# Up products of an MLP on values without 1/rms, and an attention stage with three banks for its projections

## The reference

```python
def rms_norm_2(x, g, eps=NORM_EPS):
    y = xf * lax.rsqrt(jnp.mean(xf * xf, axis=-1, keepdims=True) + eps)
    return y * g

# second_block, end of each layer l
    x = x + merged @ w_out[l]
    h2 = rms_norm_2(x, mlp_norm[l])
    x = x + jnp.square(jax.nn.relu(h2 @ w_up[l])) @ w_down[l]

# na_mixer, 16 heads of 64; the latents form a grid of 8 rows and 64 columns
    q_l, k_l, v_l = jnp.split(h_lat @ w_qkv, 3, axis=-1)
    q_c, k_c, v_c = jnp.split(h_ctx @ w_qkv, 3, axis=-1)
    # each query: a window of 8 x 16 keys with a bias, and all 256 context keys
    p = softmax([s_nb + bias, s_cx]);  o = p_nb @ v_win + p_cx @ v_c
```

## Time and profile before

| | |
|---|---|
| three timed runs | 4324.96 us median (4319.55 to 4326.48) |
| profiled execution | 4325.29 us, span 4323.5 us |
| mean granted PE clock | 0.935 |
| PE busy | 3888.6 us, 90% of the span |
| DVE busy | 1850.3 us, 43% |
| ACT busy | 1320.7 us, 31% |
| POOL busy | 432.1 us, 10% |
| DMA | 317 MB, 73 GB/s on the mean |
| chain that ended last | PE 74%, DVE 12%, ACT 6%, DMA 3%, POOL 2%, issue 2% |
| attention stage, 1348 to 1746 us | PE busy 342.1 of 398 us, clock 0.93 |
| entrance of the MLP, 2877 to 2903 us | PE busy 18.1 of 26 us, clock 0.74 |
| the same in layer 1, 3942 to 3968 us | PE busy 18.1 of 26 us, clock 0.74 |

### The profile page before, as it was taken

One profiled execution on the slowest core, in us unless ns is written; L12 is line 12 of the kernel. 1 busy time (PEld: TensorE's weight loads), 2 busy tenths in 40 slices (PEclk: granted clock), 3 DMA queues, 4 the chain that ended last, 5 costly groups with the idle time before them and its releaser, 6 DMA issues.

```text
span 4323.5 us, 52579 instructions
## 1 busy us (share of the span) xinstructions
PE 3888.6 (90%) x21392; PEld 3030.3 (70%) x21392; DVE 1850.3 (43%) x2826; ACT 1320.7 (31%) x1963; POOL 432.1 (10%) x277
## 2 busy tenths in 40 slices
PE   7788878999997899899978889899998888989999
PEld 3555546788886777688865667678886666767887
DVE  2543443533333334544444354543434435454433
ACT  3332322322223322333333331232232433123222
POOL 0211110000002110000021220000011122000000
PEclk9877878999998999899989999999999999999999
DMA  4112252121211222232211221123321121112332
GB/s 159 52 48 79 88 175 98 49 69 59 69 49 45 88 82 89 69 98 98 88 45 35 66 56 40 35 90 95 95 90 42 42 71 49 32 47 88 98 98 68
DMA packets 320320, 317.03 MB, mean 73 GB/s; under 512 B 8720, under 2 KB 286128, under 8 KB 319952
## 3 DMA queue, kind: packets, MB, share of 16 engines
q1 hardware_dynamic: 320080, 313.67, 23.0%
HBM read 311.55 MB, written 2.10 MB: 73 GB/s over the span
## 4 chain that ended last, share of the span: by engine, by line
PE 74%; DVE 12%; ACT 6%; DMA 3%; POOL 2%; issue 2%; SPq 0%; DVEq 0%; ACTq 0%; POOLq 0%
PE PS L132 74%; DVE scr L146 5%; ACT scr L142 4%; DMA ring<-in_ada_w 1%; DVE PS L160 1%; DMA scr<-in_na_bias 1%; DVE scr L156 1%; DVE NBt L156 1%; PE PS L135 1%; POOL na_w L146 1%; ACT L142 1%; DVE scr L164 1%; DVE scr L168 1%; DVE NBt L146 0%; POOL NBt L146 0%
## 5 line engine op out<-in xcount | busy, mean ns | idle before, releaser
L132 PE MATMUL PS<-scr 128*32 128x32 f32 (+7 forms) x6692 | 659.9, 284 | 131.0 <-DVE scr L146 72.8
L132 PEld LDWEIGHTS PS<-scr 128*128 128x128 f32 (+4 forms) x6692 | 538.7, 170 | 276.6 <-issue 122.5
L132 PE MATMUL PS<-ffn_h,ffn_w 128*128 128x512 f32 (+1 forms) x3168 | 616.2, 357 | 7.8 <-DVE ffn_h L156 5.7
L132 PEld LDWEIGHTS PS<-ffn_h,ffn_w 128*128 128x128 f32 x3168 | 524.8, 190 | 100.3 <-issue 9.1
L142 ACT ACTIVATE scr<-PS 128x256 f32<-128x256 f32 (+4 forms) x489 | 231.5, 473 | 1001.5 <-PE PS L132 920.6
L146 DVE TENSOR_TENSOR scr<-scr 128x512 f32<-128x512 f32 (+3 forms) x419 | 289.0, 690 | 257.9 <-ACT scr L142 221.8
L132 PE MATMUL PS<-h_h,ring_r 128*128 128x512 f32 (+1 forms) x976 | 356.1, 427 | 36.1 <-POOL ring_r L146 22.0
L132 PE MATMUL PS<-mlp_h,mlp_w 128*128 128x512 f32 x1536 | 364.3, 399 | 5.5 <-DVE mlp_h L146 5.0
L132 PE MATMUL PS<-mlp_g,mlp_w 128*128 128x512 f32 x1536 | 359.7, 396 | 0.0
L132 PEld LDWEIGHTS PS<-mlp_h,mlp_w 128*128 128x128 f32 x1536 | 291.2, 190 | 80.0 <-issue 9.5
L132 PEld LDWEIGHTS PS<-mlp_g,mlp_w 128*128 128x128 f32 x1536 | 288.5, 188 | 69.9
(11 more groups left out here) (150 smaller groups left out, 4709.6 us busy)
## 6 DMA issues: line engine op xcount, KB each, us to landing
ring<-in_ada_w SPq DMA_DIRECT2D x48, 1024.0 KB, 7.0
ring<-in_ffn_w_in SPq DMA_DIRECT2D x44, 1024.0 KB, 5.1
ring<-in_w_up SPq DMA_DIRECT2D x32, 1024.0 KB, 5.5
ring<-in_w_down SPq DMA_DIRECT2D x32, 1024.0 KB, 5.0
ring<-in_w_in SPq DMA_DIRECT2D x60, 512.0 KB, 3.9
ring<-in_ffn_w_out SPq DMA_DIRECT2D x16, 1024.0 KB, 5.1
scr<-in_na_bias SPq DMA_DIRECT2D x32, 512.0 KB, 5.5
ring<-in_na_w_qkv SPq DMA_DIRECT2D x24, 512.0 KB, 4.0
```

The costliest lines, as they stand in the source:

```text
L132: return self.eng.matmul(o, lhsT=l, rhs=r, start=start, stop=stop) if self.eng else Nothing()
```

## The change

In the MLP, `tail_act` writes `ms_at(k)[0]`, the high half of x times gain, right after each residual addition of the merge, and `tail_dve` the low half behind both additions of a group. `norm_dve` and `norm_act` are gone there. `products` gets an argument `half`, called ahead of its fifth chunk; for the first up group it is `rstd_pe`, and `rows_pe` comes behind that group. DVE copies the row into SBUF (`row`). An up tile leaves PSUM by one DVE operation, max with 0 and times row; ACT squares it and writes the high half; DVE writes the low halves after both tiles. The weight split of the second up group now stands ahead of the root and of the reciprocal.

In the attention, `flip(it)` writes into the two banks that held the scores of `it`, whose release is now the copy of the flipped probabilities; projections rotate through banks 4, 5 and 7. The order of the pieces is q, k latents, v latents, v context, k context, then the transposes of v. The split of the next q/k weights moves behind the context k on ACT and POOL, and SP makes three weight loads ahead and issues two at each `project`.

```diff
+    def products(pe, ring_, split, j, nk, segs, src, ready, full, freed, half=None):
...
         for k in range(nk):
+            if half and 2 * k == nk:
+                half()
             for t in range(nt):
...
-        for _ in range(4):
+        for _ in range(3):
             fetch()
 
         def project(tl):
             fetch()
             for _ in range(6):
-            if tl < 7:
-                fetch()
+            fetch()
...
-        s_ring, t_ring, o_ring = banks([0, 2], 2), banks([4, 5]), banks([6])
+        s_ring, o_ring = banks([0, 2], 2), banks([6])
...
-        def project(tl):
-            pe.wait_ge(*at("na_lo", "qk", tl))
-            for what, j, (t0, tn) in NQK:
+        def qk(tl, parts):
+            for what, j, (t0, tn) in parts:
...
+        def project(tl):
+            pe.wait_ge(*at("na_lo", "qk", tl))
+            yield from qk(tl, NQK[:2])
             wh, wl = w8(4096, 1024), w8(5120, 1024)
             pe.wait_ge(*at("na_lo", "v", tl))
             for s, (t0, tn) in enumerate(LC):
                 o, before = cur["rg"].take("na_made", "n_vt", tl, s)
                 emptied(pe, before)
                 for k in range(8):
...
+            yield from qk(tl, NQK[2:])
             for g in range(3):
...
-                cur["rg"] = banks([7])
-            o, before = s_ring.take("n_ex", it)
+                cur["rg"] = banks([4, 5, 7])
+            o, before = s_ring.take("n_pt", it, 1)
...
         def flip(it):
             z = it % 2
+            pe.wait_ge(*at("n_dg", it))
             for hf in range(2):
-                o, before = t_ring.take("n_pt", it, hf)
-                emptied(pe, before)
-                pe.wait_ge(*at("n_dg", it))
+                o = psum("n_pt", it, 1)[:, 512 * hf:512 * hf + 512]
                 for c in range(4):
                     t = pe.mm(o[:, c * 128:c * 128 + 128], Pm[z][:, hf, c * 128:c * 128 + 128], dg[z][:, hf, :], True, True)
                 t.then_inc(*pe.up("nt_full", it, hf))
...
-            for what, j, (t0, tn) in NQK:
-                yield
...
-            if tl < 7:
-                split_act("qk", tl + 1)
+            for what, j, (t0, tn) in NQK[:2]:
+                yield from qk(tl, what, j, t0, tn)
             for s, (t0, tn) in enumerate(LC):
...
+            what, j, (t0, tn) = NQK[2]
+            yield from qk(tl, what, j, t0, tn)
+            if tl < 7:
+                split_act("qk", tl + 1)
             for g in range(3):
...
-            o = psum("n_ex", it)
+            o = psum("n_pt", it, 1)
...
         def project(tl):
             split_pool("v", tl)
-            for _ in range(6):
+            for _ in range(10):
                 yield
             if tl < 7:
                 split_pool("qk", tl + 1)
-            for _ in range(10):
+            for _ in range(6):
...
+    row = acc[:, 0:TL]
...
-            if what == "up" and q == 0 and n == 0:
-                rstd_pe(pe, rg, f"p{l}", (LAT,), ("ss_p",))
-                rows_pe(pe, rg, f"p{l}", (LAT,))
+            first = what == "up" and q == 0 and n == 0
...
-            products(pe, rg, split, j, 8, (LOW,), src, ready, lambda t, s: (f"q{l}", j, t, s), q_freed(l, what, q, n))
+            products(pe, rg, split, j, 8, (LOW,), src, ready, lambda t, s: (f"q{l}", j, t, s), q_freed(l, what, q, n),
+                     (lambda: rstd_pe(pe, rg, f"p{l}", (LAT,), ("ss_p",))) if first else None)
+            if first:
+                rows_pe(pe, rg, f"p{l}", (LAT,))
...
         for j, (what, q, n) in enumerate(q_groups()):
             if what == "up" and q == 0 and n == 0:
+                split.act(act, j + 2)
                 rstd_act(act, f"p{l}", (LAT,))
-                norm_act(act, f"p{l}", (LAT,), None, ms_at)
             split.act(act, j + 2)
...
                 elif what == "merge" or what == "down" and q == 3 and l == 0:
                     st2 = f"p{l}" if what == "merge" else "a1"
                     act.wait_ge(*at("q_x", l, what, q, k))
+                    if what == "merge":
+                        act.f(ms_at(k, 0, TL)[0], XL[:, k, :], ACT.Identity, scale=V(f"mlp_norm{l}", k)).then_inc(*act.up("nh", st2, k, 0))
                     if k >= 3:
                         act.wait_ge(*at("ss_p", st2, k - 2, 0))
                     square_act(act, st2, k, 0, LAT, (k - 1) % 2)
                 elif what == "up":
-                    if n or q:
-                        act.wait_ge(*at("mlp_low", "q_lo", l, q if n else q - 1, (k - 2) % 8))
-                    act.f(upt[t], o, ACT.Relu).then_inc(*act.up("mlp_made", "q_up", l, what, q, k))
-                    act.wait_ge(*at("mlp_low", "q_c2", l, q, k))
+                    act.wait_ge(*at("mlp_low", "q_up", l, what, q, k))
+                    act.f(upt[t], upt[t], ACT.Square).then_inc(*act.up("mlp_made", "q_sq"))
                     if q:
                         act.wait_ge(*at(*last_down(l, q)))
                     act.f(mg_at(k, 0, TL)[0], upt[t], ACT.Copy).then_inc(*act.up("mlp_made", "q_hi", l, q, k))
...
             if what == "up" and q == 0 and n == 0:
+                split.dve(dve, j + 2)
                 rstd_dve(dve, f"p{l}", (LAT,))
-                norm_dve(dve, f"p{l}", (LAT,), lambda k, s: V(f"mlp_norm{l}", k), None, ms_at)
+                dve.wait_ge(*at("rs_full", f"p{l}", 0, "row"))
+                dve.cp(row, rstd_of(f"p{l}", 0, TL)).then_inc(*dve.up("nx", f"p{l}", 7, 0))
             split.dve(dve, j + 2)
...
                 elif what == "up":
-                    hi, lo = mg_at(k, 0, TL)
-                    dve.wait_ge(*at("mlp_made", "q_up", l, what, q, k))
-                    dve.tt(upt[t], upt[t], upt[t], ALU.mult).then_inc(*dve.up("mlp_low", "q_c2", l, q, k))
-                    dve.wait_ge(*at("mlp_made", "q_hi", l, q, k))
-                    dve.tt(lo, upt[t], hi.bitcast(F32), ALU.subtract).then_inc(*dve.up("mlp_low", "q_lo", l, q, k))
+                    dve.wait_ge(*at("pr_full", f"q{l}", j, t, 0))
+                    dve.stt(upt[t], psum(*q_freed(l, what, q, n)(t, 0)), 0.0, row, ALU.max, ALU.mult).then_inc(*dve.up("mlp_low", "q_up", l, what, q, k))
                 else:
...
+            for k in (2 * n, 2 * n + 1):
+                if what == "merge":
+                    hi, lo = ms_at(k, 0, TL)
+                    dve.wait_ge(*at("nh", f"p{l}", k, 0))
+                    dve.stt(lo, XL[:, k, :], V(f"mlp_norm{l}", k), hi.bitcast(F32), ALU.mult, ALU.subtract).then_inc(*dve.up("nl", f"p{l}", k, 0))
+                elif what == "up":
+                    hi, lo = mg_at(k, 0, TL)
+                    dve.wait_ge(*at("mlp_made", "q_hi", l, q, k))
+                    dve.tt(lo, upt[k % 2], hi.bitcast(F32), ALU.subtract).then_inc(*dve.up("mlp_low", "q_lo", l, q, k))
```

More of the change, by code:

```diff
@@ L370, in dve @@
                 self.made["dve"] = j + 1
-    def products(pe, ring_, split, j, nk, segs, src, ready, full, freed):
+    def products(pe, ring_, split, j, nk, segs, src, ready, full, freed, half=None):
         wh, wl = split.tiles(j)
@@ L1716, in na_act, with qk @@
         norm_act(act, "na", LC, ada_gain(1, 0, f_col)[1], na_parts)
+        def qk(tl, what, j, t0, tn):
+            yield
+            act.wait_ge(*at("na_in_full", "n_full", tl, j))
+            if tl >= 2:
+                act.wait_ge(*at("ns_full", 4 * (tl - 2) + 3))
+            act.f(QT[tl % 2] if what == "q" else KTt[tl % 2][:, t0:t0 + tn], psum("na_made", "n_in", tl, j)[:, 0:tn], ACT.Copy,
+                  scale=64 ** -0.5 if what == "q" else 1.0).then_inc(*act.up("na_made", "n_in", tl, j))
+            yield
         def project(tl):
```

17 lines of the change are left out of this document (6 added, 11 removed).

## The result

| | before | changed |
|---|---|---|
| median of the runs | 4323.39 us (4319.55 to 4326.48, 4 runs) | 4293.7 us (4290.82 to 4301.3, 4 runs) |
| ratio | | 0.9935, 95% interval 0.9921 to 0.9949 |
| profiled execution | 4325.29 us, span 4323.5 | 4293.35 us, span 4291.6 |
| mean granted clock | 0.935 | 0.939 |

The change makes the kernel 29.7 us faster. The forecast was 48.4 us faster, 4277 us, with a range of 4269 to 4289: the sign is right, the gain is 19 us too small (the time 17 us too long; the median of before came out 2 us lower than the forecast had it), and the time lies outside the range. The sign of being wrong that the forecast had named, a distance above 42 us in the attention, has come.

The account below looks back on a forecast made before the run. TensorE, busy 90% of the span, was taken to bound the kernel, so only its waits and half-clock stretches could pay: 4325.3 - 24.4 (MLP entrances) - 24.0 (attention) = 4276.9, said as 4277 us, range 4269 to 4289.

Parts of the forecast that it names:

- a distance above 42 us in the attention: Attention: the forecast is wrong if the distance between last value products of neighbouring head pairs stays above 42 us.
- The MLP's entrance: Both layers, PE free to second up group: 25.4 us falls to 13.2; gain 24.4 us for two (20.8 to 24.8).
- Rival B: MLP entrance: the wait returns inside the first group, half the gain is lost, 4289 us; chance 0.05.
- Steady up groups: nothing: MLP's later up groups: moving relu to DVE and the square to ACT costs nothing; 3 us if cover were gone.
- The loads: Attention: weight loads issued earlier no longer hold up bias loads, so every pair should look like the undisturbed one.
- the six distances: Attention, last value products of pairs one to seven: 264.67 us falls to 246.0, gain 18.7; lower bound 252.4, gain 12.3.
- The third bank: Attention, quarter four: v transposes need not wait for ACT's eviction; gains 1.07 us a pair of the 1.92 wait.
- the undisturbed pair: Attention: a head pair with no weight load left to issue, 42.07 us before, 41.0 forecast after the change.
- the place of POOL's split: Attention: q/k split one quarter later; POOL ends at 1675.1, PE wants it at 1677.8, margin 2.7 us, no cost.
- rival C: Attention: the q/k split moved one quarter later makes PE wait for POOL once per pair; slower, 4334 us; chance 0.03.
- new pair: 42.07 - 1.07 = 41.0: Attention: time per head pair after the change, the undisturbed pair less the third bank's gain; six make 246.0 us.
- the first pair: Attention's first head pair: last value products at 1449.1 against 1454.37, gain 5.3 us; 3.8 with half clock.

Follow-up runs that it names:

- the old order: Changed kernel with projections again q, both k, then v, and the q/k weight split back in the second quarter; 4266.44 us, ratio 0.9872.
- POOL in halves: Changed kernel with POOL's subtraction for the q/k low half cut into two instructions of half the columns; 4282.01 us, ratio 0.9914.
- the one-tensor diagonal: Changed kernel with the diagonal made by two products of the identity with a scalar per row, not one two-tensor product; 4295.86 us, ratio 0.9941.

## Why the prediction was right and wrong

**The MLP's entrance: right.** 12.55 us against 13.2. The sums took from 2873.68 to 2874.49, 0.81 (forecast 1.2), the row product 0.45 on PE's path (0.87). The gain is 25.7 against 24.4, above the upper end of 24.8 that the bounds gave. Rival B did not come: no idle row ahead of the sums. The margin for it was smaller than forecast: POOL's sum ended at 2872.84, 0.84 us ahead of PE's sums, not 1.3. "Steady up groups: nothing" holds to 0.7 us for both layers together, and the operation that takes the relu out of PSUM on DVE took 1.49 us for two (from 2882.04 on), the 0.748 of the earlier trace rows each. What the sum lacked is the 2.4 us in the unchanged code between the two MLPs.

**The loads: right in the mechanism.** SP's new order removes every wait of DVE for the bias, and the kernel with this alone shows it by itself: 16.5 us in the stage. In size it is right only together with the banks: alone it brought 6.0 of the 12.3 us that the forecast gave the six distances, because the wait for ACT that it leaves is followed by slow value products in four of six pairs.

**The third bank: right in size, with the cover named.** "The third is not worth its 1.92 us", 1.07 of it; the undisturbed pair came out at 40.94 to 40.97 against 41.0 and the remaining wait at 0.97 against 0.9, once the fault below is out of the way. What the forecast did not see is that a gone wait also takes away the half clock that sometimes followed it.

**The step that failed: the place of POOL's split, under rival C.** The forecast asked one question of the move by a quarter, whether POOL ends in time for PE: "POOL until 1675.1, and PE wants it at 1677.8", a margin of 2.7 us. It does end in time; PE never waits for na_w in the middle pairs. The second question was not asked: what DVE does from 1670.5 to 1675.1. The earlier trace rows have flips at 1672.63 in that stretch, and the trace of before has the diagonals that they wait for:

```profile
1671.89 0.42 DVE L146 TENSOR_TENSOR scr<-KC,scr 128x256 f32<-128x256 f32 x1
```

Where POOL's 4.60 us lay before, in quarter two, DVE had nothing to do; in pair two it was idle from 1477.13 to 1482.96:

```profile
1477.66 4.60 POOL L146 TENSOR_TENSOR na_w<-ring,na_w 128x2048 fp32r<-128x2048 f32 x1 [13.97 <-ACT na_w L142]
```

```profile
1482.96 0.29 DVE L164 COPY scr<-PS 128x128 f32<-128x128 f32 x1 [5.83 <-PE PS L132]
```

The forecast's term "new pair: 42.07 - 1.07 = 41.0" thus put the move of the split at nothing; in the changed kernel it costs 3.7 to 4.2 us a pair. The price is worked out from the changed kernel: the diagonal grows by 3.54 - 0.42 = 3.12 us, and the fourth quarter, from values to values, by 9.25 (1482.10 to 1491.35) against 5.73 (1473.30 to 1479.03) in the old order, which is 3.52: the flips start 2.85 us later behind the third value products, and from there to the fourth 0.67 more pass, with the flips at a lower clock. The six distances are 265.9 us against 245.7, 20.2 more: five times 3.9, and 0.7 in the last. Pair one has a slow diagonal too (1439.30) and a wait of 1.62 us for POOL, 103.9 us against 97.6: 6.3. Together 26.5, and the measured difference is 4293.7 - 4266.4 = 27.3.

With the diagonal short again the six distances are as forecast, and the rest of the attention's sum was too small: in the old order the stage is 30.5 us shorter than in before (forecast 24.0), 18.9 in the six distances (18.7), 8.6 in the first pair (5.3), and 2.9 in the last pair, which the forecast left out; 30.5 - 26.5 leaves the 4.0 of the changed kernel. So even this kernel, at 4266.4, is 11 us faster than the 4277 forecast.

Against the forecast itself the changed kernel's attention is 20.0 us short (4.0 against 24.0): 19.9 in the six distances (265.9 against 246.0) and 3.0 in the first pair (gain 2.3 against 5.3), less the 2.9 gained in the last. In the first pair the first value products came 74.6 us behind the sums, as forecast (75.0); it is the slow diagonal behind them that is missing from the sum (29.3 us to the last value products against 26.0). Rival C had the right place and the wrong mechanism: it priced a POOL that is late for PE, and 0.03 was far too little for a change that puts POOL's longest instruction somewhere else.

The trace of before showed the mechanism, in another stage. POOL and DVE there:

```profile
2428.01 2.40 POOL L146 TENSOR_TENSOR ring_r<-ring,ring_r 128x1024 fp32r<-128x1024 f32 x1 [17.23 <-ACT ring_r L142]
```

```profile
2428.52 2.17 DVE L146 TENSOR_TENSOR scr<-KC,scr 128x256 f32<-128x256 f32 x1
```

The same operation of 0.42 us takes 2.17 and ends at 2430.69, 0.28 behind POOL's 2430.41. A mean of 542 ns in its group, above the 0.42 to 0.43 of every instance in the attention stage, was the hint to follow.

The Trainium skill states the rule, in SBUF — State Buffer, "SBUF: two separate sides": DVE and GpSimd share one pair of ports, which is given to one of them for a whole instruction while the other stands still. By that rule the diagonal ends when POOL's instruction does, and a shorter instruction lets DVE in sooner; the traces agree (0.27 or 0.28 us behind POOL's end in three of them, and 1.38 in place of 3.54 us with POOL in halves). As to who competes, that section names a DVE operation with two SBUF inputs or in a mode that uses both ports; the one-tensor diagonal of 3.53 us agrees with the second, though no run here shows in which mode it ran. Not every DVE operation was held up. The reciprocal at 1483.63, on 128x2 in SBUF and beside the same POOL instruction, kept its 0.17 us:

```profile
1483.63 0.17 DVE L168 RECIPROCAL scr<-scr 128x2 f32<-128x2 f32 x1
```

DVE's copy out of PSUM at 1483.24, beside that POOL instruction too, kept its 0.29 us, and the two reductions of scores in PSUM with the bias from 1401.72 on their 0.70.

## What to carry to other kernels

When work of GpSimd is moved, ask not only whether it ends in time but beside which DVE instructions it now lies. Products, subtractions and scalings from SBUF to SBUF grew here by up to what was left of the GpSimd instruction (0.42 to 3.54 us); copies and reductions out of PSUM and a reciprocal did not. Where the engine that bounds the kernel waits for such an instruction, the growth is paid: 3.12 us of it cost 3.5 here. Put long GpSimd work where DVE idles or reads PSUM, or cut it into shorter instructions. And before forecasting, compare the mean of a group with the instances that you read: a mean above all of them says that some instance is slower, and here one of these was slowed by just this interference.

## What was not expected of the hardware

- An instruction of DVE on 2 elements per row can be kept out as well: the negation of the maxima (128x2) took 1.14 us from 1403.30 on, while POOL's 4.52 us from 1399.89 ran, in place of 0.17. The reciprocal of the same size was not (0.17 us beside POOL's 4.51).
- A scalar_tensor_tensor with two SBUF tensors in the MLP's entrance is stretched by POOL's addition of 1.30 us, from 0.75 to 1.07 us. It lies off the path there.
- A wait of 1.93 us of PE was followed by half clock in some pairs and by full clock in others of the same kernel (3.30 against 2.16 us for 24 value products), and the rows before it do not tell the two apart; this stays open.
- Runs of before lay up to 26 us apart (4310 to 4336, 19 runs), those of the old order of pieces 4 us (4 runs). In the profiled executions the attention's start varied from 1340.45 to 1352.89 us, all behind unchanged stages. Which stage varies was not followed up, so the times, unlike the rows, tell differences of 5 us only roughly.
